# Two steps of each attention piece change places on TensorE: the product with the values and the scores of three pieces later

## What is computed

```python
def chunk_causal_attention(q, k, v, q_pos, k_pos):
    s = jnp.einsum('bqhd,bkhd->bhqk', q, k) * ATTN_SCALE          # QK_DIM = 96
    visible = (k_pos[None, :] // CHUNK) <= (q_pos[:, None] // CHUNK)  # CHUNK = 64
    p = jax.nn.softmax(jnp.where(visible[None, None], s, NEG_INF), axis=-1)
    return jnp.einsum('bhqk,bkhd->bqhd', p, v)                    # V_DIM = 64
```

## Time and profile before

| | us |
|---|---|
| Median of 3 runs | 1523.77 |
| The 3 runs | 1523.75, 1523.77, 1526.86 |
| The profiled execution, its own time | 1526.47 |
| Its span in the profile | 1524.6 |
| Attention, first scores to last output | about 834.8 to 1007.2 |

### The profile page before, as it was taken

The page is one execution under the profiler, slowest core; times in us unless marked ns, Lnnn a source line. Parts: engine busy times, 40 slices in busy tenths (PEclk is TensorE's granted clock), DMA queues, the critical chain, the costliest instruction groups (busy, mean ns, idle before and its releaser), DMA issues. The chain is left out here.

```text
span 1524.6 us, 38615 instructions
## 1 busy us (share of the span) xinstructions
PE 1438.4 (94%) x16352; PEld 1001.3 (66%) x16352; DVE 838.4 (55%) x1872; ACT 494.3 (32%) x1058; POOL 153.9 (10%) x145
## 2 busy tenths in 40 slices
PE   6999999999899999999999999979997899999995
PEld 5888888885466665666655666644554677777763
DVE  3555555556768877888775665636777123222111
ACT  2222222225243444344421555544453111111110
POOL 0000000000000111011112000000000222333321
PEclk9999999999999999999999999989999899999998
DMA  9522221446232213221204643438955899999972
GB/s 334 206 98 96 96 96 68 133 142 216 72 124 88 95 56 125 67 95 52 71 23 114 172 90 87 98 120 330 335 190 190 295 337 338 346 351 354 343 246 70
DMA packets 101940, 257.65 MB, mean 169 GB/s; under 512 B 35360, under 2 KB 54448, under 8 KB 92432
## 3 DMA queue, kind: packets, MB, share of 16 engines
q1 hardware_dynamic: 94032, 237.95, 45.7%
q0 software_dynamic: 7744, 17.33, 4.9%
HBM read 203.36 MB, written 60.56 MB: 173 GB/s over the span
## 5 line engine op out<-in xcount | busy, mean ns | idle before, releaser
L559 PEld LDWEIGHTS a_ps<-a_hT,a_wz 128*128 128x128 f32 x1792 | 202.6, 192 | 6.2 <-issue 3.8
L559 PE MATMUL a_ps<-a_hT,a_wz 128*128 128x128 f32 x1792 | 204.1, 275 | 1.7 <-DMA a_wz<-w_z 1.7
L2100 PE MATMUL d_ps<-late,last_down 128*128 128x512 f32 x256 | 116.8, 603 | 1.7 <-DVE last_down L1848 1.0
L2488 DVE TENSOR_SCALAR f_y<-f_down,table 96x512 f32<-96x512 f32 x32 | 23.9, 747 | 121.2 <-PE f_down L2279 65.8
L2286 DVE COPY f_xT<-f_turned 128x384 f32<-128x384 f32 x32 | 17.8, 558 | 124.8 <-PE f_turned L2253 124.8
L2100 PEld LDWEIGHTS d_ps<-late,last_down 128*128 128x128 f32 x256 | 47.2, 192 | 52.2 <-issue 50.8
L2495 ACT ACTIVATE f_xT<-f_turned 128x384 f32<-128x384 f32 x32 | 15.7, 490 | 162.8 <-PE f_turned L2253 162.8
L1228 PE MATMUL b_ps<-r_wg,r_hT 128*128 128x512 f32 x128 | 65.7, 640 | 0.0
L1228 PE MATMUL b_ps<-b_wg,b_hT 128*128 128x512 f32 x128 | 65.4, 632 | 0.0
L471 ACT ACTIVATE a_z<-a_ps 128x512 f32<-128x512 f32 (+1 forms) x36 | 19.5, 543 | 139.5 <-PE a_ps L559 132.7
L1014 DVE STREAM_TRANSPOSE b_U<-b_T 64x256 f32<-64x256 f32 x144 | 63.3, 440 | 2.7
(11 more groups left out here) (383 smaller groups left out, 2830.7 us busy)
## 6 DMA issues: line engine op xcount, KB each, us to landing
wgu<-w_gate_up SPq DMA_DIRECT2D x15, 2048.0 KB, 35.9
late<-w_gate_up SPq DMA_DIRECT2D x9, 2048.0 KB, 40.8
wd<-w_down SPq DMA_DIRECT2D x17, 1024.0 KB, 31.1
late<-w_down SPq DMA_DIRECT2D x10, 1024.0 KB, 34.8
r_hT<-hT_d SPq DMA_DIRECT2D x16, 512.0 KB, 4.0
b_hT<-hT_d SPq DMA_DIRECT2D x16, 512.0 KB, 3.9
gate_d<-b_logits SPq DMA_DIRECT2D x32, 256.0 KB, 4.2
late<-gate_d SPq DMA_DIRECT2D x8, 1024.0 KB, 6.1
```

Of the source, the lines that this page charges most:

```text
L559: mm = pe.matmul(banks[Z_BANKS[n % 2]][:, j * P:(j + 1) * P], wz[:, i, (g + j) * P:(g + j + 1) * P], hT[t % 2][:, i, :], start=(i == 0), s ...
L2100: mm = pe.matmul(banks[2 + u][:], oT[t % 2][:, HB * branch(u) + k, :], wo[:, HB * branch(u) + k, half(u)], start=(k == 0), stop=(k == HB - 1))
```

## The change

In the body of TensorE's list the values of piece p are issued ahead of the scores of piece p + 3, instead of behind them. The number of instructions, their shapes, their buffers and all semaphore counts stay as they are. The lists of VectorE, ScalarE, GpSimd and SyncE are not touched. Where there is no piece p + 3 (the last three bodies of the unrolled round) nothing changes.

```diff
                 for p in range(ROUND):
                     if p + 1 < ROUND + ahead:
                         turn(u, p + 1)
+                    values(u, p)
                     if p + 3 < ROUND + ahead:
                         scores(u, p + 3)
-                    values(u, p)
```

## The result

The changed kernel takes 1547.96 us (median of 4 runs, 1544.7 to 1551.29), the kernel before 1523.76 us (4 runs, 1523.57 to 1526.86): so 24.2 us slower by the medians. The ratio is estimated as 1.0145, with a 95% interval of 1.0122 to 1.0169; it is not the quotient of the two medians, which is 1.0159, and by it the loss is 22.1 us (18.6 to 25.8). The sign and the mechanism were forecast, the size only in part: the sum gave 14.65 us, 1538.4 us in all. The measured median lies 2 us above the upper end of the range, 1546; by the ratio the kernel would stand right at that end, at 1545.9.

What follows compares the result with a forecast made beforehand. Attention was taken as bound by the run from wide scores over maximum and exponential to the wide turn. Values' slots added 14.65 us, other terms 0, to the median 1523.77: 1538.4 us, range 1531 to 1546.

Steps and rivals of the forecast that it cites:

- What bounds: In attention, the run from wide scores over maximum and exponential to the wide turn bounds: 2.42 us for 768 columns.
- The slots of the values: Wide turns of tiles 6, 5, 4, next 7 wait longer by the preceding values' slots: 14.65 us in all.
- Junctions: Where values now directly precede scores, changeovers equal the old ones in sum: 0 us, bounds -4 and +4 us.
- The clock: Rival, 8%: tile 7's wait of 1.49 us lowers TensorE's clock, 12 us over 7 heads on top, 1550.4 us.
- The accumulator wait: Values directly behind a wide turn find the accumulator bank read out: 0 us, margin 0.03 us, at most 6 us.
- Narrow pieces at no cost: Narrow turns lose cover but still have 2.1 us of other TensorE work ahead: no cost.
- Faster, ScalarE's list set free: Rival, 5%: values issued sooner let ScalarE start wide exponentials sooner, at most 6.9 us gained, 1516.9 us.

Runs made afterwards that it cites:

- With the chain relieved: Kernel before with scores of p + 3 ahead of turn of p + 1 and VectorE's maximum ahead of its copy: 1523.58 us, ratio 0.9985; repeated 0.9994.
- on_chain: Kernel before with values ahead of scores only at places 1, 3, 6 and 8, where the next wide piece's scores are put off: 1552.14 us, ratio 1.0166.
- the split kernel: Kernel before with only the first key block of the values ahead of the scores at places 1, 3, 6 and 8: 1540.63 us, ratio 1.0094.

## Why the prediction was right and where it fell short

- **What bounds.** Right: the run from wide scores over maximum and exponential to the wide turn. The swaps off that chain cost 4 us by themselves, those on it by themselves as much as the whole change. One part was not seen: how near TensorE's own work lies to that bound. With the chain relieved a head falls only from 20.92 or 21.00 to 20.6 or 20.8 us, so both bounds lie side by side.
- **The slots of the values** (0.62, 0.27, 0.38, 0.73). Right as terms and in their counts, 14.65 us of the 24.2. With a single block of values moved, each further block costs 0.11 or 0.12 us: from `on_chain`'s growth to that of the split kernel it is 0.34 us less for three blocks fewer (tile 6) and 0.12 for one (tile 4).
- **Junctions.** This is the step that failed most: "I take the new junctions equal in sum to the old ones", with bounds of 4 us either way. They measured 0.19, 0.19, 0.20 and 0.25 us an interval, 0.83 us a head and 6.2 us in all, beyond the bound of 4. The bound was my guess of 0.1 us for one junction; each swap makes two, and they add. The single block shows the constant by itself: 0.46 us, of which 0.03 us for each of its 4 records is work.
- **The clock.** The rival came true in part: one lowered stretch in seven waits of 1.45 us, 2.2 us, where the rival had it at all of them. Its condition, a length of wait from which the clock falls, is not what the traces show: at 1.64 us it fell at six of seven such turns in one kernel (10.7 us in its trace) and at two of seven in another (3.6 us), and at 2.62 us once not at all. The sum should have held one or two such stretches instead of none.
- **The tail.** It has no term in the sum: the last unrolled round still puts off the scores of the last tile 3, and its turn waits, 0.7 us. The count stopped at the wide turns.
- **The accumulator wait.** Right for the changed kernel (one wait of 0.8 us at the end, where before there were two, 0.9 us in all), and the margin was real: the kernels in which place 5 is not swapped have that 0.20 us in every head.
- **Narrow pieces at no cost.** Nearly: the swaps off the chain cost 0.40 us a head of the loop when alone.
- **Faster, ScalarE's list set free.** Its condition, an output step that ends after the maximum, was not met. The wait for values fell from 46.5 to 1.5 us, and it gave nothing.

The sum with measured terms is 14.65 + 6.2 + 2.2 + 0.7 = 23.8 us. It describes the profiled execution, whose distance is 24.9 us between spans; the medians give 24.2 us and the ratio 22.1. The runs of the changed kernel spread over 6.6 us (1544.7 to 1551.29), as much as the junctions' term, so the terms rest on the intervals of the traces and not on the medians.

## What to carry to other kernels

Ahead of swapping two steps on an in-order engine, find which of them feeds a fixed run on other engines that the same engine later waits for. That step goes first, and the other one is cover behind it: moved ahead, it costs its whole slot. Add the junctions, two for each swap, and leave room for the clock where the resulting waits grow: behind some of the waits of 1.45 and 1.64 us here TensorE ran at half clock, which cost 1.3 to 2.9 us each time, about as much as the wait or more. And an operation that waits less is no gain as long as another input of its successor comes later still.

## What the runs showed of the hardware that was not expected

A wait of 1.64 us, with TensorE busy 0.66 us of the 2.30 ahead of its end, was followed by half clock for 3.4 us or more at six of seven such turns in one kernel, and filling 0.9 us of it with useless transposes took 13 us off the kernel's distance to the kernel before. In another kernel the same wait, with the same 0.66 us of 2.30, was followed by it at two of seven, so the wait alone does not decide it. Waits of 1.45 us did so once in seven, in each of two executions. And 2 small matmuls put between a turn and scores cost 0.46 us, four times the 0.12 us of their work.
